# Where the weights' high parts and the expert rows are placed, and the output sums by column groups and 128 tokens, in a hybrid decoder block

## The reference

```python
u = rms_norm(h, norm1_g);  proj = u @ w_in
y_conv = conformer_conv(proj[..., :1024]) ; y_attn = moba_attention(q, k, v) @ w_attn_out
mixed = g[..., :D] * y_conv + g[..., D:] * y_attn
h = h + mixed @ w_out                       # w_out 1024 x 1024
u2 = rms_norm(h, norm2_g)
logits = u2 @ w_router + b_router           # 32 experts
top_v, top_i = top_k(logits, 4); gates = softmax(top_v)
# for each expert e, for its tokens:
hid = u2[tok] @ w_ug[e] + b_ug[e]           # 1024 x 2048, 8 MiB
act = min(a, 7) * sigmoid(1.702 a) * (clip(lin) + 1)
y = act @ w_down[e] + b_down[e]             # 1024 x 1024, 4 MiB
h = h + gate * y                            # 32 experts x 12 MiB
```

## Time and profile before

| | us |
|---|---|
| median of 3 runs (lowest, highest) | 1074.58 (1074.17, 1075.23) |
| the profiled execution's own time | 1074.9 |
| its span, first to last instruction | 1073.2 |
| PE busy | 891.8 (83% of the span) |
| DVE busy | 440.1 (41%) |
| ACT busy | 255.1 (24%) |
| bytes moved by DMA | 432.96 MB, mean 403 GB/s |

### The profile page before, as it was taken

One profiled execution on the slowest core, in us unless ns is written; L12 is line 12 of the kernel. 1 busy time (PEld: TensorE's weight loads), 2 busy tenths in 40 slices (PEclk: granted clock), 3 DMA queues, 4 the chain that ended last, 5 costly groups with the idle time before them and its releaser, 6 DMA issues.

```text
span 1073.2 us, 18590 instructions
## 1 busy us (share of the span) xinstructions
PE 891.8 (83%) x6874; PEld 402.9 (38%) x6875; DVE 440.1 (41%) x1109; ACT 255.1 (24%) x413; POOL 6.2 (1%) x36
## 2 busy tenths in 40 slices
PE   9999999996765689699956999978996956997557
PEld 8889996331221123233311333322331311332112
DVE  6998985432222224244412344432442312343222
ACT  5478744121111111022201122221111201112111
POOL 2000000000000000000000000000000000000000
PEclk9999999998788889899988999998998988999898
DMA  9964689999999999999999999999999999999997
GB/s 325 391 204 127 247 353 397 412 435 429 431 431 432 432 431 430 431 431 435 434 430 432 430 434 431 431 431 431 432 435 431 431 431 434 431 431 431 430 425 305
DMA packets 33718, 432.96 MB, mean 403 GB/s; under 512 B 3109, under 2 KB 5569, under 8 KB 18976
## 3 DMA queue, kind: packets, MB, share of 16 engines
q1 hardware_dynamic: 33168, 431.99, 95.6%
q10 hardware_dynamic: 528, 0.66, 0.2%
HBM read 431.59 MB, written 1.05 MB: 403 GB/s over the span
## 4 chain that ended last, share of the span: by engine, by line
PE 57%; DMA 32%; another core or an unknown queue 4%; SPq 3%; DVE 1%; ACT 1%; issue 1%; DVEq 0%
PE bank L1623 22%; PE bank L1662 11%; DMA down_odd<-in_w_down 10%; DMA up_odd<-in_w_up_gate 9%; DMA down_even<-in_w_down 8%; PE bank L1306 6%; DMA up_even<-in_w_up_gate 4%; PE bank L1603 3%; PE bank L1244 3%; PE bank L1537 3%; PE bank L1524 3%; PE bank L1349 2%; SPq L532 2%; SPq L536 1%; DMA down_odd<-in_w_in 1%
## 5 line engine op out<-in xcount | busy, mean ns | idle before, releaser
L1623 PE MATMUL bank<-up_even,reg_r 128*32 128x512 f32 x1472 | 194.0, 679 | 80.4 <-DMA up_even<-in_w_up_gate 79.8
L1623 PE MATMUL bank<-up_odd,reg_r 128*32 128x512 f32 x1408 | 182.5, 672 | 67.9 <-DMA up_odd<-in_w_up_gate 67.9
L1200 DVE SCALAR_TENSOR_TENSOR ys<-bank,gslot,ys 64x512 fp32r<-64x512 f32 x90 | 67.4, 749 | 231.0 <-ACT ys L803 229.6
L803 ACT ACTIVATE ys<-bank,gslot 64x512 fp32r<-64x512 f32 x90 | 61.5, 683 | 317.8 <-PE bank L1662 316.7
L1623 PEld LDWEIGHTS bank<-up_even,reg_r 128*32 128x32 f32 x1472 | 50.6, 123 | 216.0 <-issue 127.6
L1623 PEld LDWEIGHTS bank<-up_odd,reg_r 128*32 128x32 f32 x1408 | 48.4, 122 | 199.1 <-issue 121.3
L797 ACT ACTIVATE reg_m<-reg_m 128x256 f32<-128x256 f32 x45 | 18.8, 418 | 418.8 <-DVE reg_m L1179 418.8
L1662 PE MATMUL bank<-down_odd,reg_r 128*32 128x512 f32 x704 | 83.4, 606 | 14.3 <-DMA down_odd<-in_w_down 14.3
L1662 PE MATMUL bank<-down_even,reg_r 128*32 128x512 f32 x736 | 83.7, 595 | 9.2 <-DMA down_even<-in_w_down 9.0
L1179 DVE TENSOR_SCALAR reg_m<-bank 128x256 f32<-128x256 f32 x45 | 19.1, 425 | 158.2 <-PE bank L1623 158.2
L849 DVE TENSOR_TENSOR w_lo<-down_even,w_hi 128x2048 fp32r<-128x2048 f32 x24 | 55.0, 2304 | 8.3 <-ACT w_hi L634 8.2
(11 more groups left out here) (279 smaller groups left out, 1014.1 us busy)
## 6 DMA issues: line engine op xcount, KB each, us to landing
up_odd<-in_w_up_gate SPq DMA_DIRECT2D x29, 4096.0 KB, 46.5
up_even<-in_w_up_gate SPq DMA_DIRECT2D x28, 4096.0 KB, 39.7
down_even<-in_w_down SPq DMA_DIRECT2D x15, 4096.0 KB, 42.5
down_odd<-in_w_down SPq DMA_DIRECT2D x14, 4096.0 KB, 46.8
down_even<-in_w_in SPq DMA_DIRECT2D x16, 1024.0 KB, 6.1
up_odd<-in_w_up_gate SPq DMA_DIRECT2D x10, 1024.0 KB, 10.5
up_even<-in_w_up_gate SPq DMA_DIRECT2D x4, 2048.0 KB, 13.8
up_even<-in_w_up_gate SPq DMA_DIRECT2D x6, 1024.0 KB, 8.4
```

Source lines behind the costliest of these rows:

```text
L803: nc.scalar.activation(ys[0:64, half, :], YB[r, :], ACT.Identity, scale=gslot[r, :]).then_inc(y_high, 1)
L1200: nc.vector.scalar_tensor_tensor(ys[64:P, half, :], YB[r, :], gslot[0:64, :], ys[0:64, half, :].bitcast(F32), ALU.mult, ALU.subtract).then ...
L1623: ins = mm(UP[q * SLOTS:(q + 1) * SLOTS, :], XT[:, k, :], up_columns(a, k, q), start=False, stop=(k == KD - 1), skip_group_check=True)
```

## The change

It does five things. (1) The second half of the convolution's matrix and all of `w_out` have their high parts in tile 1 alone (three half places in all), so row 1 of expert 0 goes out right after the convolution's second half; the conversion of the second half of i = 11 then waits until that place is free, and stands later in ACT's and DVE's programs. (2) An output bank holds columns 4n to 4n + 3 of every group of eight (`columns`), so the moving operand reads runs of 4 floats with steps of 8, and a bank pair is enough for four feature blocks. (3) The last quarter runs bank by bank with the transposes between, per column group and 128 tokens. (4) The logits are made with the turned tokens as stationary operand (128 columns) and the router matrix as moving one (32 columns): no parts, no copies, no matmul with `pick`; `pos` and `hot` are made per 128 tokens. (5) Rows are loaded and used in the first tile in the order `FIRST_ROWS`, row 2 last, and expert 2's rows are sent as these rows come free.

```diff
+FIRST_ROWS = 0, 1, 4, 6, 7, 3, 5, 2
+        def columns(t, n):
+            return t.rearrange("p (f c) -> p f c", c=KD)[:, :, 4 * n:4 * n + 4]
+        def high_half(i, b):
+            if i < CONV_W:
+                return w_hi[i % 2][:, 2048 * b:2048 * b + 2048]
+            if (i, b) == (CONV_W, 0):
+                return w_hi[0][:, 0:2048]
+            column = 2048 * (1 - b)
+            return w_hi[1][:, column:column + 2048]
@@ sync
             load_half(CONV_W, 1)
+            load_first_row(1)
             sp.wait_ge(pv_done, HEADS)
...
-            for b in range(2):
-                load_half(OUT_W + 1, b)
-                load_first_row(b)
+            load_half(OUT_W + 1, 0)
+            load_first_row(0)
+            load_half(OUT_W + 1, 1)
             sp.wait_ge(mix_ready, 4)
...
             out_used(sp, 2)
-            load_first_row(2)
+            load_first_row(3)
             load_down(0, 2, 3, 0)
             load_first_row(5, 0, FF)
-            sp.wait_ge(out_eighth, 1)
-            load_first_row(3, 0, FF)
-            load_down_columns(0, 6 * D, 7 * D, 0)
             out_used(sp, 3)
-            load_first_row(3, FF, 2 * FF)
             load_first_row(5, FF, 2 * FF)
-            load_down_columns(0, 7 * D, 8 * D, 0)
+            load_first_row(2)
+            load_down(0, 3, 4, 0)
@@ fetch_third_up
-                for first, end, c, done in ((0, 1, 0, up_row[0]), (1, 2, 0, up_row[1]), (2, 4, 0, up_done[0]),
-                                            (4, 6, 1, up_done[1]), (6, 8, 1, up_done[1])):
-                    sp.wait_ge(done, items)
+                for j, k in enumerate(FIRST_ROWS):
+                    if k == 6:
+                        continue
+                    sp.wait_ge(up_row[j] if j in up_row else up_done[j // UPK], items)
+                    first, end = (6, 8) if k == 7 else (k, k + 1)
@@ scalar
+            full(act, U_ATT + 1)
             weights_high(CONV_W, 1)
             full(act, U_ATT + 3)
-            for b in range(2):
-                weights_high(OUT_W, b)
+            weights_high(OUT_W, 0)
             for b in range(4):
                 act.wait_ge(mix_ready, b + 1)
                 if b == 2:
                     full(act, U_CONV + 3)
+                    weights_high(OUT_W, 1)
@@ vector
             mix_low(1)
+            mix_add(3)
             weights_low(OUT_W, 1)
-            mix_add(3)
...
             add_to_h(0, 0)
+            add_to_h(0, 1)
+            turned_half(0, 0)
             add_to_h(1, 0)
-            add_to_h(0, 1)
-            turned_half(0)
+            turned_half(1, 0)
             add_to_h(1, 1)
-            dve.wait_ge(std2, 1)
-            copy_parts(0)
-            turned_half(1)
+            rstd_of(0)
+            turned_half(1, 1)
...
+            biased(0)
             largest(0)
-            copy_parts(1)
             choose(0)
-            dve.wait_ge(logits_second, 1)
-            step(biased(1, bank[U_LOG % 4][:, E:2 * E]))
+            rstd_of(1)
+            biased(1)
             largest(1)
             choose(1)
             nc.vector.tensor_scalar(st[:, 16:18], top[:, :, 0, 0], -1.0, None, ALU.mult).then_inc(v0_ready, 1)
+            place_tokens(0)
+            place_tokens(1)
@@ tensor
-                        ins = mm(bank[u % 4][:], m_r[x][j][:, k, m * P:(m + 1) * P], w[y][:, k, 512 * n:512 * n + 512],
+                        ins = mm(bank[u % 4][:], m_r[x][j][:, k, m * P:(m + 1) * P], columns(w[y][:, k, :], n),
...
+            def logits(m, b):
+                freed(pe, U_U2T + 2 * b + m)
+                for j in range(4):
+                    ins = mm(LOGITS[m], u2T_half(m, b)[:, j, :], wr[:, 4 * b + j, :], start=(b == 0 and j == 0), stop=(b == 1 and j == 3))
+                return ins
...
+            out_product(3, 0, 0)
+            out_product(3, 0, 1)
+            transpose_h(0, 0)
+            out_product(3, 1, 0)
+            transpose_h(1, 0)
+            out_product(3, 1, 1)
+            transpose_h(0, 1)
+            pe.wait_ge(wr_ready, 1)
+            logits(0, 0)
+            transpose_h(1, 1)
+            logits(0, 1).then_inc(logits_full, 1)
+            logits(1, 0)
+            logits(1, 1).then_inc(logits_full, 1)
...
             pe.wait_ge(bup_in, 64)
             bias(0)
+            clear(0)
+            pe.wait_ge(tab_ready, 1)
+            claim(U_TAB)
+            mm(bank[U_TAB % 4][:, 0:E], tri[:], msk[:, 0, :], start=True, stop=True).then_inc(bank_full[U_TAB % 4], 1)
+            claim(U_TAB + 1)
+            mm(bank[(U_TAB + 1) % 4][:, 0:E], ones[:], msk[:, 0, :], start=True, stop=False)
             pe.wait_ge(tab_ready, MT)
+            mm(bank[(U_TAB + 1) % 4][:, 0:E], tri[:], msk[:, 1, :], start=False, stop=True).then_inc(bank_full[(U_TAB + 1) % 4], 1)
...
+            gather(GA, lambda m: pe.wait_ge(hot_built, m + 1))
+            clear(1)
...
-                for k in range(KD):
+                for j, k in enumerate(FIRST_ROWS if first else range(KD)):
```

More of the change, by code:

```diff
@@ L248, in hybrid_block @@
         up_in = [[sem(f"up_in{a}_{c}") for c in range(UPS)] for a in range(2)]
-        up_row = [sem(f"up_row{k}") for k in range(2)]
+        up_row = {j: sem(f"up_row{j}") for j in (0, 1, 2, 4, 5, 6)}
         first_row = [sem(f"first_row{k}") for k in range(7)]
@@ L1032, in add_to_h, with build_hot @@
                 full(dve, u)
-                hs = hx[:, m, n * 512:(n + 1) * 512]
-                nc.vector.tensor_tensor(hs, hs, bank[u % 4][:], ALU.add).then_inc(bank_free[u % 4], 1)
-            def build_hot(slot, e):
-                for m in range(MT):
+                hs = columns(hx[:, m, :], n)
+                nc.vector.tensor_tensor(hs, hs, bank[u % 4][:].rearrange("p (f c) -> p f c", c=4), ALU.add).then_inc(bank_free[u % 4], 1)
+            def build_hot(slot, e, tokens=range(MT)):
+                for m in tokens:
                     nc.vector.tensor_scalar(hot[:, m, :], slot, pos[:, m, e], st[:, 6 + m:7 + m], ALU.is_equal, ALU.mult).then_inc(hot_built, 1)
@@ L1115, in _ @@
             nc.vector.tensor_copy(cum[0:1, T_LEAD:T_LEAD + 1], exp_col[0:1, 0:1]).then_inc(lead_ready, 1)
-            dve.wait_ge(expg, 2 * MT)
-            step(nc.vector.reciprocal(st[:, 18:20], st[:, 18:20]))
-            for m in range(MT):
-                nc.vector.scalar_tensor_tensor(gate[:, m, :], ev[:, m, :], st[:, 18 + m:19 + m], msk[:, m, :], ALU.mult, ALU.mult).then_inc(gate_ready, 1)
             def rows_turn(n, rows):
@@ L1131, in _ @@
             rows_scale(0)
+            dve.wait_ge(expg, 2 * MT)
+            step(nc.vector.reciprocal(st[:, 18:20], st[:, 18:20]))
             full(dve, U_WIDE)
@@ L1140, in _ @@
             freed(dve, U_WIDE)
+            for m in range(MT):
+                nc.vector.scalar_tensor_tensor(gate[:, m, :], ev[:, m, :], st[:, 18 + m:19 + m], msk[:, m, :], ALU.mult, ALU.mult).then_inc(gate_ready, 1)
             full(dve, U_KEYS)
@@ L1526, in gather @@
                 ins.then_inc(gathered, 1)
-            pe.wait_ge(tab_ready, 1)
-            claim(U_TAB)
-            tb = bank[U_TAB % 4]
-            mm(tb[:, 0:E], tri[:], msk[:, 0, :], start=True, stop=True)
-            mm(tb[:, E:2 * E], ones[:], msk[:, 0, :], start=True, stop=False)
             def bias(n):
@@ L1655, in tile @@
                 if not last:
-                    pe.wait_ge(down_in[a][0], 16 * pair + (32 if a == 1 else 80))
+                    pe.wait_ge(down_in[a][0], 16 * pair + (32 if a == 1 else 64))
                 order = [(r, half) for r in range(KD - 2) for half in range(2)] + [(r, half) for half in range(2) for r in (KD - 2, KD - 1)]
```

172 lines of the change are left out of this document (64 added, 108 removed).

## The result

Seven runs of the changed kernel took 1074.27 to 1078.65 us, median **1078.13**, seven of the kernel before beside them 1074.17 to 1075.23, median 1074.88. The ratio is 1.0022, with an interval of 1.0013 to 1.0032: slower by a little over 0.2%, where 1073.7 us and "same" were forecast. (The ratio goes with the means, 1077.19 and 1074.76 us; the medians are 0.30% apart.) The seven times are not one heap: two lie at 1074.3 and five between 1077.98 and 1078.65. The execution that was profiled is the slowest of them, 1078.65 us, with a span of 1076.9.

The account below looks back on a forecast made before the run. The end is set by when expert 2's first row is asked for (S), then a fixed weight stream at 431 GB/s. -0.55 - 0.3 = -0.85 us from 1074.9 gives 1074.05, as median 1073.7 us; range 1072.2 to 1077.4.

Parts of the forecast that it names:

- parts 3 and 4: Last quarter of output products through logits and tables to the first row of matmuls: S moves by -0.55 us.
- S: Moment when expert 2's first row is asked for, 184.79 us before; claimed to set the end.
- rival A: The 96 output products: strided operand costs 36 ns each or more, time 1077.2 us or up to 1087.5; chance 0.13.
- Rival C: Logit matmuls: weights load more slowly, 32 take 3.7 us, S within 0.1 us of now, time 1074.3; chance 0.20.
- Part 1: Row 1 loaded earlier and i = 11's conversion later: price 0, with 1.2 us to spare before PE needs it.
- the freed megabyte: Row 1's earlier transfer fills the hole at 140 to 142 us: 2.4 us of cover, worth nothing by itself.
- Part 2: Strided columns in the 96 output products: taken as 0, bounds 0 to 3.5 us.
- Part 5: Order and release of rows in the first tile: 0.3 us gained behind S, bounds 0 and 0.6.
- the third issue: SP's load of expert 2's third megabyte, after three rows instead of four, about 1.2 us earlier relative to S.

Follow-up runs that it names:

- e5: The changed kernel again, unaltered: ten runs from 1073.53 to 1075.11 us and two at 1077.50 and 1077.86.
- e7: e1 with row 1 asked for at its old place, behind the last half of w_out: 1075.03 us.
- e3: The kernel before with only the strided columns of the output products, adds and squares strided too: 1075.01 us, ratio 1.0004.
- e8: e4 with the high parts of w_out stored in the order in which they are read: 1074.49 us, ratio 1.0001.
- e12: e1 with expert 2's rows released as before the change, not one by one: 1074.80 us, ratio 0.9999.
- e2: The kernel before with its four wide products moved from between the logits to just ahead of the first tile: 1074.89 us, ratio 1.0000.
- e6: The changed kernel with two wide products moved between the groups of logits: 1074.62 us, ratio 0.9999.
- e11: The changed kernel again, unaltered: eight runs from 1073.83 to 1074.64 us and four from 1077.00 to 1079.07.
- e10: e9 with a wide product after about every eight narrow logit matmuls, the two late ones taken out: 1082.73 us.
- e4: The changed kernel with the logits made as before, by parts and pick, wide products between: 1075.25 us, ratio 1.0005.
- e9: The changed kernel with 14 of its 16 narrow logit matmuls issued a second time into an unread bank: 1083.81 us.
- e1: The changed kernel with a wide product of 128 x 256 behind each of the four groups of logits: 1074.88 us, ratio 1.0000.

## Why the prediction was wrong

**The step that failed** is in parts 3 and 4, the tail of the chain: every term from the logits to the first row of matmuls was priced from rows at a granted clock of 1.00, and a fall of the clock was put at nothing without a reason. S was to move by -0.55 us and moved by +3.27 in the execution profiled, which is also beyond the 1.2 us that the prediction named as a sign of being wrong. Its only word on the clock is that the 24 output products would run at 1.00, and they did; the fall came behind them. The change swapped 128 moving columns for 32, took the wide products out from between them, and so made a stretch from 175.2 to 179.4 us that is only narrow matmuls and four transposes. The clock fell in it, and the fall is worth 3.9 us of S in the execution profiled; judging by the times, 11 of 31 runs fell, and the medians of the two groups are 4.0 us apart. None of the rivals named the clock. That about a third of the runs would be slower by some 0.3% belonged in the rivals, with the price that the rows allowed: bias(0), the gather and the first row are 0.94 + 1.07 + 1.07 = 3.1 us of PE's work, and the tables come on top, all at half the pace.

The Trainium skill ("TensorE: Matmul & The Clock Gate", section "The HAM clock gate (the "warmup" mystery)" of its Part 1) lets the clock go by how busy PE has been, and says of the rise to the full clock that its moment varies from run to run of the same kernel, since the monitor doesn't start with the kernel. Of a fall in mid-kernel it doesn't say so; the two groups of the 31 runs would fit. By the first, read with the busy column, no fall was to be expected: PE is busy for 2.00 of 2.00 us in both stretches around it. The measurement decides; a full busy column isn't enough.

**With the clock held, the steps stand.** e5, the same program at 1.00, term by term:

```
                              forecast   e5
start of the last quarter     168.0      168.21 (151.40 + 72 x 0.2334)
24 output products            5.45       5.60
16 transposes                 2.24       1.83 (0.44 + 0.44 + 0.44 + 0.51)
32 logit matmuls              3.1        3.41 (0.81 + 2.60)
end of the logits on PE       178.8      179.04
XT's turn begins              182.15     182.08
S                             184.24     184.17
behind S (span - S)           888.1      888.5
```

S is right to 0.1 us, with the help of errors that cancel, and of luck: the output products of this execution started 0.26 us earlier than in the one that the forecast was made from. From their start S was to come 32.58 us later (184.24 - 151.66) and came 32.77 later. The strided columns cost 0.46 ahead of the last quarter and 0.15 in it; the logits cost 0.107 each, not 0.098; and the transposes 0.11 each, not 0.140. The 0.140 was a wrong reading: 1.12 us is the time from the first start to the last end, while the packed 0.104 was taken from start to start. From 175.78 to the start of the next matmul,

```profile
176.75 0.31 PE L1512 MATMUL bank<-pick,reg_r 128*128 128x32 f32 x2
```

the eight take 0.97 us, 0.121 each. So the 36 ns that rival A was priced by were 17.

Rival C had the logits right in kind. The estimate of 3.4 us from the Trainium skill ("TensorE: Matmul & The Clock Gate", section "LDWEIGHTS (loading the stationary operand)"), which the prediction set aside for the rows at 93 and 104 ns, is what was measured, 3.41.

**Part 1** held. In the changed kernel's first profile the late conversion ran on ACT at 151.56 (L641, 1.91 us) and on DVE at 153.50 (L851, 2.29 us), to 155.8, ahead of PE's need at 157.1, and the chain of the changed kernel is output products without a gap. SP's two loads behind `mix_ready` and `mix_lo` went out at 153.11 and 157.03, forecast 153.3 and, for `mix_lo`, 157.3. The price of 0 for the freed megabyte is borne out by e7.

**Part 2** was mis-sized: 0 taken, 0.6 us measured (e3, e8), inside its bounds of 0 to 3.5.

**Part 5**: 0.3 us taken, none seen, and so small a term isn't resolved. Span minus S is 888.4 before and 888.2 to 888.5 for the changed kernel at the full clock, and e12, with the old releases, has 888.4. The low rate at 188 to 190 us doesn't hang on the third issue: with the old releases that stretch moves 315 GB/s in the kernel before, 336 in e12 and 406 in e2, with the new ones 299 in e6, 328 in e11, 340 in e5 and 389 in e7. In the kernel before its share of 1.04 says that packets took longer, and not that the queue was empty.

So the mended sum is: S - start from 33.13 to 32.77, -0.36 us, after the strided columns have taken 0.6 back; nothing resolved behind S; and where the clock falls, +3.9. The 20 runs of the lower group have their median at 1074.36, 0.5 under the 1074.88 of the 98 runs of before, but they are picked by their time, so that this is no clean measure. All that the four kernels with wide products have is a ratio of 0.9999 or 1.0000, each within 0.0010. **No version that ran is shown to be faster than the kernel before**: no interval lies below 1.

What stays open: why the clock falls in some runs and not in others, and why 5 of 7 runs were slow in the first session, 2 of 12 in the second and 4 of 12 in the third, which may be chance or the chip; whether e10's later fall is owed to its wide products or to luck, since one execution of either was profiled; whether the 4 of 98 runs of before at 1077 us and more, and the three of e3, e4 and e8, are falls as well; and whether it is the 32 columns or only the length of the stretch that matters, since no run has logits of 128 columns for as long.

## What to carry to other kernels

A matmul rewritten so that fewer columns move per weight load can keep PE's busy time whole and still lose its clock, so price the work behind a stretch of narrow matmuls at both levels, the more so where a chain (here S) hangs on it, and read the granted clock of every stretch before and after. If a narrow stretch of some microseconds can't be avoided, a few wide products between them were cheap here (0.2 us each, 0.12 us of S for two), but look at the clock again when the stretch grows: e10 fell with them. And when a few runs of a kernel fall in two heaps, get more runs and a profile of each heap before explaining the median or trusting the interval of one session.

## What was not expected of the hardware

- The granted clock went from 1.00 to 0.50 while PE was busy without a gap (176 to 180 us of the changed kernel: 2.00 of 2.00 in both stretches, by the profile's modelled ends), amid 32 fp32 matmuls of 32 moving columns; in the kernel before without its wide products, PE idle for 0.25 and 0.43 us of 2.00 and 128 columns moving in the logits, it stayed at 1.00.
- Once low, it stayed so for 10 us (178.6 to 188.9) in the changed kernel and 17 us (178.0 to 195.0) in e9, PE busy all the time; it came back in both, and in e10, during the first tile's matmuls of 512 moving columns.
- Products of 256 columns whose operands are all zero stood between the narrow matmuls in e1, e6, e7 and e12, where the clock stayed at 1.00 in the four executions profiled.
- At the low clock the pairs with 512 moving columns took 1.87 us for 0.94, and a row of eight 1.87 for 1.07.
- Runs of four floats with steps of eight as moving operand cost 6.4 ns in a product of 512 columns (0.2334 us in the changed kernel and 0.2333 in e3, against 0.2270).
